# A hybrid decoder layer on one core: the opening reordered, other bank and eviction orders at the norms, transposes in place of broadcast products, a narrow unit of 16 columns, and more filler ahead of the block inverses

## What is computed

```python
mod = silu(c) @ w_ada + b_ada                        # 9 x 1024 numbers: shift, scale, gate for each part
u = rms_norm(h, g_ffn1) * (1 + sc1) + sh1
h = h + 0.5 * gt1 * ((silu(u @ Wa) * (u @ Wb)) @ w_ffn1_out)
u = rms_norm(h, g_mix) * (1 + sc2) + sh2
q_sb,k_sb,v_sb, q_dn,k_dn,v_dn,z_dn, b_dn,a_dn, r_sb,r_dn = split(u @ w_in)
y_sb = stick_breaking_attention(qk_norm(q_sb), qk_norm(k_sb), v_sb) @ w_up_sb
q,k,v = l2_norm / silu of a causal 4-tap convolution of q_dn,k_dn,v_dn
beta = sigmoid(b_dn);  g = -exp(a_log) * softplus(a_dn + dt_bias)
o = gated_delta_rule(q, k, v, g, beta)               # blocks of 64: a triangular inverse in each
y_dn = (rms_norm(o, g_dn_out) * silu(z_dn)) @ w_up_dn
h = h + gt2 * ((sigmoid(r_sb) * y_sb + sigmoid(r_dn) * y_dn) @ w_out)
out = h + 0.5 * gt3 * swiglu(rms_norm(h, g_ffn2) * (1 + sc3) + sh3)
```

## Time and profile before

| | us |
|---|---|
| median of 3 runs | 1258.53 |
| the runs | 1256.99, 1258.69, 1258.53 |
| the profiled execution's own time | 1256.85 |
| its span, first to last instruction | 1255.1 |
| PE busy in it | 1233.3 |

### The profile page before, as it was taken

The page is one execution under the profiler, slowest core; times in us unless marked ns, Lnnn a source line. Parts: engine busy times, 40 slices in busy tenths (PEclk is TensorE's granted clock), DMA queues, the critical chain, the costliest instruction groups (busy, mean ns, idle before and its releaser), DMA issues.

```text
span 1255.1 us, 18298 instructions
## 1 busy us (share of the span) xinstructions
PE 1233.3 (98%) x6665; PEld 1003.7 (80%) x6665; DVE 693.1 (55%) x998; ACT 624.8 (50%) x1142; POOL 62.2 (5%) x96
## 2 busy tenths in 40 slices
PE   7999999999999999999999999999999999999998
PEld 5788888888888688777778888877788888888887
DVE  4566666675664884887683665566733333332221
ACT  5577676775553756666854344444422222231221
POOL 0000000001110000000211110003000000000000
PEclk9999999999999999999999999999999999999999
DMA  9666666675554232212221213643233333243330
GB/s 350 196 198 180 201 200 181 185 203 158 162 154 114 67 101 68 67 51 68 68 89 40 77 36 104 198 147 89 68 111 90 99 100 99 88 129 101 109 86 25
DMA packets 278039, 152.41 MB, mean 121 GB/s; under 512 B 8005, under 2 KB 273374, under 8 KB 277982
## 3 DMA queue, kind: packets, MB, share of 16 engines
q1 hardware_dynamic: 273552, 149.46, 40.8%
q10 hardware_dynamic: 4430, 2.17, 0.6%
HBM read 145.31 MB, written 6.29 MB: 121 GB/s over the span
## 4 chain that ended last, share of the span: by engine, by line
PE 90%; ACT 4%; DVE 4%; issue 1%; ACTq 0%; DVEq 0%
PE tail L1645 13%; PE tail L1647 13%; PE tail L1646 13%; PE region L1645 13%; PE region L1647 13%; PE region L1646 13%; PE region L1914 1%; PE region L2070 1%; DVE w_lo L1066 1%; ACT w_hi L590 1%; PE region L2074 1%; PE region L1897 1%; PE region L1948 1%; DVE u_lo L1188 1%; PE region L1813 1%
## 5 line engine op out<-in xcount | busy, mean ns | idle before, releaser
L590 ACT ACTIVATE w_hi<-raw 128x1024 fp32r<-128x1024 f32 (+1 forms) x177 | 197.3, 1115 | 422.5 <-PE region L1647 214.5
L1066 DVE TENSOR_TENSOR w_lo<-raw,w_hi 128x1024 fp32r<-128x1024 f32 (+1 forms) x177 | 229.5, 1296 | 214.1 <-ACT w_hi L590 213.1
L1645 PE MATMUL region<-u_hi,w_hi 128*128 128x512 f32 x672 | 262.6, 391 | 1.7 <-DVE u_lo L1188 0.8
L1646 PE MATMUL region<-u_lo,w_hi 128*128 128x512 f32 x672 | 261.7, 389 | 0.0
L1647 PE MATMUL region<-u_hi,w_lo 128*128 128x512 f32 x672 | 261.6, 389 | 0.0
L1645 PEld LDWEIGHTS region<-u_hi,w_hi 128*128 128x128 f32 x672 | 126.1, 188 | 30.7 <-DVE u_lo L1188 2.0
L1645 PE MATMUL tail<-u_hi,w_hi 128*128 128x512 f32 x360 | 146.5, 407 | 2.8 <-DVE w_lo L1066 1.3
L1647 PEld LDWEIGHTS region<-u_hi,w_lo 128*128 128x128 f32 x672 | 126.1, 188 | 26.3
L1646 PEld LDWEIGHTS region<-u_lo,w_hi 128*128 128x128 f32 x672 | 126.1, 188 | 26.2
L1647 PE MATMUL tail<-u_hi,w_lo 128*128 128x512 f32 x360 | 140.5, 390 | 0.0
L1646 PE MATMUL tail<-u_lo,w_hi 128*128 128x512 f32 x360 | 140.3, 390 | 0.0
(11 more groups left out here) (342 smaller groups left out, 1467.9 us busy)
## 6 DMA issues: line engine op xcount, KB each, us to landing
raw<-in_w_ffn_in SPq DMA_DIRECT2D x168, 256.0 KB, 3.4
ada_raw<-in_w_ada SPq DMA_DIRECT2D x56, 512.0 KB, 4.9
raw<-in_w_in SPq DMA_DIRECT2D x90, 256.0 KB, 3.3
raw<-in_w_ffn_out SPq DMA_DIRECT2D x32, 384.0 KB, 5.0
raw<-in_w_ffn_out SPq DMA_DIRECT2D x32, 320.0 KB, 4.1
ada_early<-in_w_ada SPq DMA_DIRECT2D x8, 1024.0 KB, 9.7
gates<-kept_gates SPq DMA_DIRECT2D x16, 256.0 KB, 4.0
raw<-in_w_out SPq DMA_DIRECT2D x16, 256.0 KB, 3.1
```

What stands on the lines that cost most here:

```text
L590: act.activation(w_hi[:, slot % 2, 0:k, :], raw[:, slot, 0:k, :], ACT.Copy).then_inc(hi_ready, 1)
L1066: dve.tensor_tensor(w_lo[:, slot % 2, 0:k, :], raw[:, slot, 0:k, :], w_hi[:, slot % 2, 0:k, :].bitcast(f32), ALU.subtract).then_inc(lo_rea ...
L1645: pe.matmul(bank(b), wh, xh, start=start and n == 0, stop=False)
L1646: pe.matmul(bank(b), wh, xl, start=False, stop=False)
```

## The change

The diff touches seven places. The core of it:

```diff
 FILL:   "prep": 10  ->  "prep": 13
 # SP and ACT, opening: the six DMAs of vec2_rows go from ACT's queue to the end of SP's early queue
+            sp.dma_start(vec2_rows[0:48, :], w_conv[0].rearrange("t (k p) -> (t k) p", p=P)).then_inc(rates_in, 16)
+            ...
-            act.dma_start(vec2_rows[0:48, :], w_conv[0].rearrange("t (k p) -> (t k) p", p=P)).then_inc(small_in, 16)
...
+            act.preload_act_table_set("silu_and_others")
             act.wait_ge(masks, 10)
...
-            act.preload_act_table_set("silu_and_others")
             act.wait_ge(vec_ps, 1)
-            act.activation(vec[:, :], bank(6)[:, 0:96], ACT.Copy).then_inc(vec_ready, 1)
-            act.activation(vec2[:, :], bank(6)[:, 128:179], ACT.Copy).then_inc(vec_ready, 1)
-            act.activation(ones_r[:, :], ones[:, :], ACT.Copy)
-            act.activation(mean_64r[:, :], mean_64[:, :], ACT.Copy)
-            act.wait_ge(tok_ps, 1)
-            act.activation(rstd[:, :], bank(4), ACT.Copy).then_inc(rstd_ready, 1)
+            act.activation(vec[:, :], bank(5)[:, 0:96], ACT.Copy).then_inc(vec_ready, 1)
...
             early_part(0)
+            act.wait_ge(tok_ps, 1)
+            act.activation(rstd[:, :], bank(4), ACT.Copy).then_inc(rstd_ready, 1)
             early_part(1)
...
+            act.wait_ge(vec_ps, 2)
+            act.activation(vec2[:, :], bank(6)[:, 0:51], ACT.Copy).then_inc(vec_ready, 1)
             ffn(0, F1_IN)
 # PE, opening: piece 0, then the spread by transposes, then totals 0 and piece 1; one identity product fewer
+            pe.wait_ge(vec_ready, 1)
             early_piece(0)
+            pe.wait_ge(tok_step, 4)
+            for b in range(NB):
+                ins = pe.transpose(bank(4)[:, b * P:(b + 1) * P], tok["rstd"][:, b:b + 1].to_broadcast([P, P]),
+                                   ident[:, :])
+            ins.then_inc(tok_ps, 1)
+            early_totals(0)
             early_piece(1)
...
-            for b in range(2):
-                pe.matmul(bank(b), ident[:, :], x_nat[:, b, 0:S], start=True, stop=True)
+            pe.matmul(bank(0), ident[:, :], x_nat[:, 0, 0:S], start=True, stop=True)
...
+            pe.wait_ge(rates_in, 16 * 8)
+            pe.transpose(bank(6)[:, 0:51], vec2_rows[:, :], ident[0:51, 0:51]).then_inc(vec_ps, 1)
             ffn_in(0, F1_IN)
 # DVE, norm(s)
-                dve.wait_ge(tok_ps, 1 + s)
-                scaled(s, 0, bank(4))
-                scaled(s, 1, bank(4))
+                dve.wait_ge(rstd_ready, 1 + s)
+                scaled(s, 0, rstd[:, :])
+                scaled(s, 1, rstd[:, :])
+                if s == 1:
+                    evict(0)
                 split_lo(late(s), 0, 2)
-                if s == 1:
-                    dve.tensor_copy(rstd[:, :], bank(4)).then_inc(rstd_ready, 1)
-                    evict(0)
...
                 low(s, KD - 1)
+                if s == 1:
+                    evict(1)
 # PE, late_units and the units behind them
                     if k == 3:
                         statistics(s)
+                    if k == 5:
+                        spread_root(s)
                     if k == KD - 1:
                         pe.wait_ge(u_lo_ready, plain + KD)
-                        spread_root(s)
...
-            late_units(1, (6, 7, 6, 7))
+            late_units(1, (6, 7, 4, 5))
 # PE, the ba unit: one weight tile that holds the high part in 8 columns and the low part in the next 8
+            def narrow():
+
+                pe.wait_ge(proj_ready, 12 - 1)
+                pe.wait_ge(lo_ready, DN_IN + 1)
+                for k in range(KD):
+                    both = w_hi[:, DN_IN % 2, k, 0:4 * DNH]
+                    pe.matmul(bank(6)[0:4 * DNH, :], both, u_hi[:, k, :], start=k == 0, stop=False)
+                    ins = pe.matmul(bank(6)[0:4 * DNH, :], both, u_lo[:, k, :], start=False, stop=k == KD - 1)
+                ins.then_inc(unit_done, 1)
...
-                ins = pe.transpose(bank(3)[:, 8 * b:8 * b + 8], ab_T[:, b * P:(b + 1) * P], ident[0:8, 0:8])
+                ins = pe.matmul(bank(3)[:, 8 * b:8 * b + 8], ab_T[:, b * P:(b + 1) * P], pick[:, :],
+                                start=True, stop=True)
 # PE, delta net
-                        ins = pe.matmul(region[e][:, h * P:(h + 1) * P],
-                                        small["g"][:, b, h:h + 1].to_broadcast([P, P]), upto[:, :],
-                                        start=True, stop=True)
+                        ins = pe.transpose(region[e][:, h * P:(h + 1) * P],
+                                           small["gsum"][:, b, h:h + 1].to_broadcast([P, P]), ident[:, :])
...
+                if pair == 0:
+                    key_products(0)
+                    pe.wait_ge(nat_ready, 1)
+                    sums(0)
+                    pe.wait_ge(l2_ready, 8)
+                    sums(1)
+                    pe.wait_ge(nat_ready, 3)
+                    key_products(1)
+                    pe.wait_ge(nat_ready, NB)
 # ACT and DVE, delta net: the fills stand one level later
-                fill("inv0")
-                if pair:
-                    fill("norm")
                 for l in range(1, JOIN + 1):
...
-                    fill("level")
+                    if l == 1:
+                        fill("inv0")
+                        if pair:
+                            fill("norm")
+                    else:
+                        fill("level")
...
+                fill("level")
                 fill("join")
 # DVE, MERGE
-                    split_lo(MERGE, i, oo + 2)
                     dve.wait_ge(branch_lo, DNH + o)
...
                     dve.tensor_tensor(ssq[:, :], ssq[:, :], rstd[:, :], ALU.add).then_inc(sum_ready, 1)
+                    split_lo(MERGE, i, oo + 2)
                     dve.wait_ge(m_hi_ready, o + 1)
```

More of the change, by code:

```diff
@@ L64 @@
 SHADOW = {"keep": 18, "weights": 3, "y": 3}
-FILL = {"silu": 12, "l2": 8, "start": 8, "prep": 10, "inv0": 2, "norm": 4, "level": 2, "join": 1, "solve": 2, "solved": 5, "step": 1, "carry": 1,
+FILL = {"silu": 12, "l2": 8, "start": 8, "prep": 13, "inv0": 2, "norm": 4, "level": 2, "join": 1, "solve": 2, "solved": 5, "step": 1, "carry": 1,
         "last": 2}
@@ L793, in _ @@
             for n in range(12):
+                if n == 1:
+                    split_hi(SB_IN, 0, 4)
                 if n < 2:
@@ L2030, in _ @@
                     ins.then_inc(kk_ps, 1)
+                if pair == 0:
[7 more added lines that the diff above has]
+                    pe.wait_ge(nat_ready, NB)
+                else:
+                    for b in both:
+                        pe.wait_ge(o_ready, b - 1)
+                        pe.wait_ge(state_ready, b - 1)
+                        pe.wait_ge(v_new_ready, b - 1)
+                        sums(b)
+                        key_products(b)
                 for b in both:
```

119 lines of the change are left out of this document (64 added, 55 removed).

## The result

The changed kernel is slower: 1265.72 us (median of 4, 1265.23 to 1266.65) against 1258.57 (1256.99 to 1258.69), ratio 1.0057, 95% interval 1.0046 to 1.0069. The forecast was 1254.0 with a range up to 1257.8. The profiled execution has a span of 1263.9 us, 8.8 more than before; it ran in 1265.66, next to the median.

What follows compares the result with a forecast made beforehand. PE was taken as the bound, busy 1233.3 of 1255.1 us. Terms -0.65 + 2.5 - 3.15 - 1.82 + 0.7 - 1.25 - 0.85 = -4.5 us gave 1254.0 from 1258.53; range 1249.3 to 1257.8.

Steps and rivals of the forecast that it cites:

- norm(1), the units behind it and the narrow unit: First norm and following units: cheaper spread and fewer waits, -3.15 us; narrow unit with 16 matmuls for 24, -1.82.
- MERGE and norm(2): MERGE's wait for m_lo goes, -1.25 us; second norm's cheaper transposes and shorter u_lo wait, -0.85.
- Handover: Start of feed-forward block: ACT waits for a late PE transpose, block begins 3.2 us later, some won back; +2.5 us.
- Delta net: Spreads and waits save 4.0 and 2.2 us; new units' splits ahead of the inverse cost 3.95 and 2.9; total +0.7.
- Opening: Root chain's work comes forward, but the fourth early-weights piece's landing lets only 0.6 us past; -0.65 us.
- SP's queue ahead of it is untouched, so I don't expect it: Opening: the fourth early piece's landing was not expected to move; if it did, the gain would be up to -1.4 us.
- B: Rival: PE's clock falls in one or two of the new waits, about 1.95 us each; 1256 to 1258, chance 0.19.
- C: Rival: clock falls in all three new waits and again behind the second pair's, 7.8 us; 1261.8, chance 0.05.
- the 2.6 us of rows 3 (L1775) cost no clock: Opening: PE's 2.6 us wait for the root's chain showed no clock fall; the new waits are all longer.
- 1.95: Price in us of one clock fall, from 3.9 us at half speed read off the opening's slow transposes of x.
- against the profiled execution: Whole kernel: all terms counted against the profiled run, giving 1252.35 us, that run being 1.7 us under the median.

Runs made afterwards that it cites:

- experiment 3: Changed kernel with the new tile pick put in the place of share, so every other tile has its address of before; 1260.45 us.
- c_best4: Changed kernel with vec2 transposed early, first-pair prep fill parted 8 and 7, second 12, 320 unused bytes ahead of hT and 192 ahead of vec; 1245.00 us.
- Experiment 5: Changed kernel with PE's transpose of vec2 moved ahead of the last pair of half products; 1262.74 us.
- experiment 7: Kernel before with two needless products on PE in the opening's wait of 2.6 us; 1256.88 us.
- experiment 1: Kernel before with only an unused tile of 32 bytes per partition allocated ahead of vec; 1263.77 us, ratio 1.0047.
- experiment 6: Changed kernel with the addresses of before, plus three needless products on PE in the handover wait; 1258.13 us against 1260.45.

## Why the prediction was wrong, step by step

Time between places of PE's timelines, in us, for the kernel before, that with 32 bytes, the changed one, the changed one with the old addresses (experiment 3), and c_best4:

| from ... to | before | 32 bytes | changed | exp. 3 | c_best4 |
|---|---|---|---|---|---|
| 0 ... first output product of block 1 | 274.39 | 276.12 | 279.25 | 278.87 | 274.15 |
| ... norm(1) | 124.12 | 125.83 | 125.79 | 124.12 | 122.42 |
| ... transposes of v (attention) | 83.35 | 83.47 | 78.81 | 78.62 | 78.54 |
| ... delta net | 121.47 | 121.38 | 122.04 | 122.11 | 121.95 |
| ... MERGE's output product | 231.85 | 232.06 | 236.33 | 238.46 | 228.76 |
| ... output product of block 2 | 291.34 | 292.06 | 290.70 | 289.40 | 289.72 |
| ... last instruction | 125.26 | 127.51 | 127.51 | 125.26 | 124.24 |

- *norm(1), the units behind it and the narrow unit*, -3.15 - 1.82 = -4.97: measured -4.7 with the old addresses. Right. 0.6 us are lost again in the attention (121.47 to 122.1), which the sum didn't have.
- *MERGE and norm(2)*, -1.25 - 0.85 = -2.1: -1.9. Right.
- *Handover*, 3.2 us of idle time: 3.25. Right. The chain is the one that was worked out (copy at 51.86, `w_lo` from 53.12, product from 54.26). Experiment 5 shows that it hangs on the place of that transpose.
- *Delta net*, waits of 3.95 and 2.9 us: 4.09 and 2.91. Sum +0.7: in the changed kernel +4.5, of which 3.4 are two clock falls, so +1.1. Right but for the clock.
- *Opening*, -0.65: with the old addresses the fourth piece starts at 21.11 us in place of 22.0, bound by its landing as said, and PE gets through the opening 0.7 us earlier (49.92 for 50.62). In the changed kernel the piece starts at 22.75. The step "SP's queue ahead of it is untouched, so I don't expect it" named the queue as the only thing that could move the landing; the target's address moved it, to the other side.
- **The first step that failed: the clock's price was in a rival and not in the sum.** All three waits cost a fall, 5.1 us in the profile. No rival had just this: B had one or two falls, up to 1258, and C (0.05) had all three and a fourth, 1261.8; three at its price are 5.85 us, 1259.9, between them. The argument against it was "the 2.6 us of rows 3 (L1775) cost no clock". By experiment 7 they did cost one in about half of the executions of before (36 of 67 runs over 1258); the profile had happened to show the other kind. The two groups of times stood in the three runs shown, 1256.99 against 1258.69 and 1258.53, 1.6 us apart, near the 1.95 that the prediction itself put on a fall. I took this for scatter and added it to the forecast as a constant. The Trainium skill, "TensorE: Matmul & The Clock Gate", Part 1, calls the throttled state the default, which activity releases; the changed kernel's profile agrees, with a fall at each of the three waits (0.83, 0.83, and 0.91 with 0.92), and was nearer to this than to the row. The price itself, 1.95, was read from slow transposes between 5 and 7 us, where the granted clock reads 1.00 in the row below, so only their length spoke for the lower level; by the windows a fall cost 1.7 here, and up to 3.4 in experiment 3.

```profile
5.00:7.00 2.00, 1.78 (x9) 1.78 (x10) 0.63 (x1) 1.97 (x3) 0.00 (x0) 1.00 1.01 391
```

- **The second: "against the profiled execution" the untouched work was taken as unchanged.** The new tile appears in the diff and was costed at nothing, with no row named as its cover. It cost 6.8 us of span in experiment 1 (5.3 in the medians), the largest term of all, and no rival had it. By the table 1.7 of it lies ahead of the first output product, where the early pieces land later, and 4.9 in the stretches whose matmuls read g or MERGE's `m`.
- Either of the two would by itself have carried the time past the top of the range, 1257.8: 1254.0 with the 5.1 us of the clock is 1259.1, with the 5.3 us of the address 1259.3.

The account closes to 0.3 us: the span of experiment 3 is 5.1 us longer than before, with clock losses of 3.4, 3.4 and 1.7 in its profile, so without the clock the change is worth -3.4 (forecast -4.5). With 5.1 of the clock as in the changed kernel's profile and 6.8 of the address this is +8.5, of 8.8 measured in the spans. The medians differ by 1.7 less, because, by experiment 7, the run in the middle of before holds a fall that its profiled execution doesn't.

## What to carry to other kernels

Look at the addresses of an allocation's neighbours when a tile is added, however small: a kernel that is full of matmuls can be 5 us slower by 32 bytes, and a window in which nothing was changed, with PE busy throughout, is where it shows. A wait of PE of two to four microseconds, or two shorter ones close together, costs its idle time and, in part of the executions, a clock fall of 1.7 us or more beside; two groups of run times are the sign, and a single profile shows only one of them. Where a fill is lengthened, follow the unit boundaries inside it: the split that a new unit needs must stand ahead of the step that the other engines wait for.

## What the runs showed of the hardware

- The rate of 128 x 512 matmuls on split float32 went by where the moving tile begins against where the weights begin, counted against 512 bytes: 0.227 us where they are equal (192 and 192, 0 and 0), 0.229 to 0.230 with the moving tile at 0 and the weights at 192, 0.233 with it at 32, 64 or 128. PE shows neither idle time nor a lower clock for it. Why is open, and other pairs weren't tried.
- DMAs of 1 MB into a tile at a multiple of 512 landed in 9.5 to 9.8 us (median), into one 32 to 192 bytes past it in 10.6 to 11.1; the rate between 10 and 20 us was 385 and 348 to 350 GB/s.
- PE's clock fell to the lower level (1.2 GHz) in profiles at waits of 2.1, 2.3, 2.9, 3.3 and 4.1 us, and at one of 1.76 that began 1.4 us behind one of 0.96. It held in profiles through waits of 2.3, 2.6 and 2.8 us at the opening, and the wait of 2.6 us cost a fall in about half of the executions. Needless products in such a wait, two in the one of 2.6 us (listed with 1.98 us) and three in the one of 3.25 us (2.84), kept it up; the runs were then all but one in the lower group of before (experiment 7), and 1.6 to 2.3 us faster (experiment 6).
